# A hybrid decoder step on one core: key chunks, scores and rows in another order

## The reference, cut

```
h = RMSNorm(x);  z = h @ W_in + b_in -> q | k | v | cv_a | cv_g
A = MoBA attention(q, k, v)      8 heads x 64, blocks of 256, own block + the top 3 by q . mean(k)
C = silu(LayerNorm(causal dwconv31(cv_a * sigmoid(cv_g)))) @ W_pw
x = x + RMSNorm(concat[A, C] @ W_out)
u = RMSNorm(x) @ W_up            2 x 2816 wide
x = x + RMSNorm((silu(gate) * val of causal dwconv3(u)) @ W_down)
```

## Time and profile before

| | us |
|---|---|
| median of 3 runs | 1104.83 |
| lowest and highest | 1099.54, 1115.49 |
| the profiled execution's own time | 1101.12 |
| its span | 1099.3 |
| TensorE busy | 972.2 (88%) |
| VectorE busy | 701.6 (64%) |
| ScalarE, GpSimd busy | 444.2, 456.4 |

### The profile page before, as it was taken

How to read it: one execution, slowest core, us unless ns; L and a number is a source line. 1 busy time by engine, 2 the same in 40 slices (tenths; PEclk the granted TensorE clock), 3 DMA queues, 4 the chain that set the end, 5 groups by cost and what they waited for, 6 DMA issues and landing times.

```text
span 1099.3 us, 19605 instructions
## 1 busy us (share of the span) xinstructions
PE 972.2 (88%) x7520; PEld 710.7 (65%) x7520; DVE 701.6 (64%) x920; ACT 444.2 (40%) x892; POOL 456.4 (42%) x408
## 2 busy tenths in 40 slices
PE   3988987889797876977989878999999999999995
PEld 3546663455454444545645558999999999667663
DVE  3689685767665474687432547888888889523115
ACT  3325554656564655444231223333333333234332
POOL 1014445547462848351000335545555545333430
PEclk9998998989897687998999998999999999999998
DMA  9897798997979763787966211232222231222222
GB/s 322 294 320 250 283 332 299 313 358 274 337 260 334 249 216 130 250 283 247 390 181 188 77 39 39 84 103 83 78 78 77 80 113 39 77 77 77 77 73 86
DMA packets 155207, 205.19 MB, mean 187 GB/s; under 512 B 10097, under 2 KB 75634, under 8 KB 155072
## 3 DMA queue, kind: packets, MB, share of 16 engines
q1 hardware_dynamic: 154619, 202.33, 55.1%
q10 hardware_dynamic: 495, 1.62, 0.5%
HBM read 198.59 MB, written 5.68 MB: 186 GB/s over the span
## 4 chain that ended last, share of the span: by engine, by line
PE 63%; SPq 14%; DVE 8%; issue 4%; DMA 4%; ACT 3%; POOL 2%; POOLq 0%; DVEq 0%; ACTq 0%
SPq L326 7%; PE tp L894 7%; PE z L894 6%; PE sc L894 6%; PE z L749 5%; SPq L313 4%; PE ob L894 3%; PE sm L894 3%; PE sc L537 3%; PE tp L925 3%; DMA kN<-in_cache_k 3%; PE ob L925 3%; PE ob L597 2%; PE z L925 2%; PE z L619 2%
## 5 line engine op out<-in xcount | busy, mean ns | idle before, releaser
L1858 POOL TENSOR_TENSOR conv<-conv,prod 128x576 f32<-128x576 f32 x120 | 174.3, 1452 | 143.7 <-ACT prod L1109 130.0
L1453 DVE STREAM_TRANSPOSE kT<-kN 128x2048 f32<-128x2048 f32 x64 | 145.5, 2294 | 52.4 <-DMA kN<-in_cache_k 51.9
L1904 POOL TENSOR_TENSOR wulo<-wu,wuhi 128x2048 fp32r<-128x2048 f32 x22 | 102.3, 4650 | 14.5 <-ACT wuhi L1179 14.5
L1108 ACT ACTIVATE prod<-glu,consts 128x512 f32<-128x512 f32 x124 | 88.9, 717 | 44.8 <-POOL conv L1858 41.8
L1922 POOL TENSOR_TENSOR wdlo<-wd,wdhi 128x1024 fp32r<-128x1024 f32 x22 | 57.4, 2609 | 90.0 <-ACT wdhi L1384 90.0
L537 PE MATMUL sc<-kT,qS 128*32 128x256 f32 x1024 | 70.4, 422 | 26.3 <-DVE kT L1453 23.7
L1763 DVE TENSOR_TENSOR fTlo<-fT,fThi 128x1152 fp32r<-128x1152 f32 x22 | 29.8, 1356 | 91.5 <-ACT fThi L1383 91.5
L632 PE MATMUL z<-hT,wz 128*128 128x512 f32 x192 | 87.1, 607 | 0.0
L597 PE MATMUL ob<-vN,pT 128*32 128x128 f32 x2048 | 75.9, 301 | 0.0
L1043 ACT ACTIVATE S<-sc 128x512 f32<-128x512 f32 x32 | 35.0, 1095 | 98.5 <-PE sc L537 98.4
L597 PEld LDWEIGHTS ob<-vN,pT 128*32 128x32 f32 x2048 | 61.8, 144 | 18.0 <-issue 15.7
(11 more groups left out here) (313 smaller groups left out, 2549.3 us busy)
## 6 DMA issues: line engine op xcount, KB each, us to landing
kN<-in_cache_k SPq DMA_DIRECT2D x256, 256.0 KB, 4.5
vN<-in_cache_v SPq DMA_DIRECT2D x256, 256.0 KB, 4.0
wu<-in_w_up SPq DMA_DIRECT2D x44, 512.0 KB, 4.6
wd<-in_w_down SPq DMA_DIRECT2D x22, 512.0 KB, 3.6
wz<-in_w_in SPq DMA_DIRECT2D x20, 512.0 KB, 6.9
wo<-in_w_out SPq DMA_DIRECT2D x1, 4096.0 KB, 16.4
xA<-in_x_prompt SPq DMA_DIRECT2D x4, 512.0 KB, 11.6
wq<-in_w_in SPq DMA_DIRECT2D x1, 2048.0 KB, 17.6
```

The costliest lines, as they stand in the source:

```text
L1108: act.activation(dst[:, 0:TP_], glu[:, i, j:j + TP_], ACT.Copy, scale=w_cv[:, i, j:j + 1])
L1453: dve.transpose(kT[:, u % 4, :, :].rearrange("p c (i k) -> p i c k", i=4), kN[:, c % 3, :, :].rearrange("p i (c k) -> p i c k", k=32)).the ...
L1858: pool.tensor_tensor(conv[:, i, :], conv[:, i, :], prod[:, n % 2, :], ALU.add).then_inc(s["prod_used"], 1)
L1904: pool.tensor_tensor(wulo[f % 2][:, :, :], wu[f % 2][:, :, :, :].rearrange("p k u n -> p k (u n)"), wuhi[f % 2][:, :, :].bitcast(F32), ALU ...
```

## The change

The order of SyncE's queue: the fourth chunk of keys, 8b+19, is loaded together with 8b+16 to 8b+18, ahead of the values 8b+8 to 8b+11 (at the start 8 to 11 in place of 8 to 10), and keys 8b+13 before values 8b+4. In samples 0 to 3 scores(b+1, 3) follow scores(b+1, 2) directly, at u = 2; ScalarE's copies follow. VectorE turns keys 8(b+2) before the last reduce_scores in place of after penalize; glu_values(2) moves behind that reduction. 106 taps in place of 98 come before sample 4. Of a head's four rows the widest is scaled on VectorE, in p_sums, with a semaphore pnorm_w of its own. Two heads' products with the values run together, alternating between the halves of the partitions (pv_pair), behind the second head's turn. mix_squares(0) stands before exps(7), its root is split off as mix_root, and its sum on VectorE is split off as mix_sum. The order of W_out tiles is 0, 1, 2, 4, 3 (AT); the last turn_out writes bank SC0.

The diff, cut; left out are the same replacement of t by AT[t] in more waits, and mix_sum and mix_root taken out of mix_rows and mix_squares.

```diff
@@ -274,15 +274,17 @@
         wd_full = [s[f"wd_full{i}"] for i in range(4)]
         HEADS_AT = {4: 0, 5: 4}
         XO = (4, 0, 1, 2, 3)
+
+        AT = (0, 1, 2, 4, 3)
         TILES = [(what, i) for i in range(4) for what in "vk"] + [("q", i) for i in range(4)]
         TILES_AT = {1: 0, 2: 4, 3: 8}
-        TAPS_FIRST, TAPS_HEADS = 98, (5, 3, 3)
+        TAPS_FIRST, TAPS_HEADS = 106, (5, 3, 3)
         def scores_at(b):
-            return (0, 2, 2, 3) if b < 4 else (0, 2, 3, 4)
+            return (0, 2, 2, 2) if b < 4 else (0, 2, 3, 4)
...
@@ -357,19 +359,20 @@
             for c in range(4):
                 load_v(c)
             load_wz(2)
-            for c in range(8, 11):
+            for c in range(8, 12):
                 load_k(c)
             rows = lambda n: a[n][0, 0].rearrange("(t p) h d -> p t (h d)", p=P)
             for b in range(NB):
                 if b < NB - 1:
-                    load_k(8 * b + 11)
                     load_k(8 * b + 12)
                 if b < 4:
                     load_wz(2 * b + 3)
+                if b < NB - 1:
+                    load_k(8 * b + 13)
                 load_v(8 * b + 4)
                 if b < NB - 1:
-                    for c in range(8 * b + 13, 8 * b + 16):
-                        load_k(c)
+                    load_k(8 * b + 14)
+                    load_k(8 * b + 15)
                 else:
                     sp.wait_ge(s["kt_ready"], NB * SUPER)
                     sp.dma_start(histF[0:16, :], a["state_ffn"][0].rearrange("b w n -> (b w) n")).then_inc(s["histf_loaded"], 16)
...
@@ -402,7 +405,7 @@
                     sp.wait_ge(s["glun_done"], 2)
                     sp.dma_start(wpw[:, :, :], a["w_cv_pw"][0].rearrange("(k p) n -> p k n", p=P)).then_inc(s["wpw_loaded"], 16)
                 if b < NB - 2:
-                    for c in range(8 * b + 16, 8 * b + 19):
+                    for c in range(8 * b + 16, 8 * b + 20):
                         load_k(c)
                 if b == 6:
...
@@ -600,9 +603,8 @@
             def turn_out(b):
                 pe.wait_ge(s["o_norm"], b + 1)
-                if b == NB - 1:
-                    pe.wait_ge(s["h2_raw"], 3)
-                pe.transpose(TB0[:, 0:P], oN[:, :], ident).then_inc(s["ot_done"], 1)
+                bank = SC0 if b == NB - 1 else TB0
+                pe.transpose(bank[:, 0:P], oN[:, :], ident).then_inc(s["ot_done"], 1)
...
@@ -683,7 +685,8 @@
                     pe.matmul(bank[:, n - P:n], ident16, causal16, start=False, stop=True).then_inc(s["ps_done"], 1)
             def t_head(h):
-                pe.wait_ge(s["pnorm"], 4 * h + 4)
+                pe.wait_ge(s["pnorm"], 3 * h + 3)
+                pe.wait_ge(s["pnorm_w"], h + 1)
                 if h == 0:
                     pe.wait_ge(s["glun_put"], 2)
...
@@ -704,17 +707,20 @@
                 return sum(TP_ - P * i for i in range(kb))
-            def pv_head(h):
-                hp, e = h // 2, h % 2
-                if h == 0:
+            def pv_pair(hp):
+
+                if hp == 0:
                     pe.wait_ge(s["s_put"], 20)
-                if hp and e == 0:
+                else:
                     pe.wait_ge(s["o2_put"], hp)
+                pe.wait_ge(s["ptt_put"], 8 * hp + 8)
                 for kb in range(4):
-                    pe.wait_ge(s["ptt_put"], 4 * h + kb + 1)
-                    ins = pe.matmul(SC1[64 * e:64 * e + 64, kb * P:TP_], vP[:, kb, h * DH:(h + 1) * DH],
-                                    pPT[:, h % 2, turned(kb):turned(kb) + TP_ - kb * P], start=(kb == 0), stop=(kb == 3))
-                ins.then_inc(s["pv2_done"], 1)
+                    for e in range(2):
+                        h = 2 * hp + e
+                        ins = pe.matmul(SC1[64 * e:64 * e + 64, kb * P:TP_], vP[:, kb, h * DH:(h + 1) * DH],
+                                        pPT[:, e, turned(kb):turned(kb) + TP_ - kb * P], start=(kb == 0), stop=(kb == 3))
+                        if kb == 3:
+                            ins.then_inc(s["pv2_done"], 1)
             def statistics(what, done, banks):
...
@@ -734,8 +740,10 @@
             def mix_half(t, nh, part):
                 m = tok(t)
-                if part == 0 and t:
-                    pe.wait_ge(s["t1_put"], 2 * (t - 1) + nh + 1)
+                if part == 0 and t == 3:
+                    pe.wait_ge(s["m4_put"], nh + 1)
+                elif part == 0 and t:
+                    pe.wait_ge(s["t1_put"], 2 * (AT[t] - 1) + nh + 1)
                 if t == 4:
                     for e in range(2):
...
@@ -813,16 +821,14 @@
                     elif u == 2:
                         t_head(h)
                     elif u == 3:
-                        pv_head(h)
                         s_head(h + 2)
                     elif u == 4:
                         t_head(h + 1)
                     elif u == 5:
-                        pv_head(h + 1)
+                        pv_pair(h // 2)
                         s_head(h + 3)
                     elif u == 6:
                         t_head(h + 2)
-                        pv_head(h + 2)
                     elif b == 4:
                         pe.wait_ge(s["pexp"], 16)
                         pe.wait_ge(s["conv_done"], CT)
...
@@ -877,13 +883,14 @@
                             if u == scores_at(b)[j]:
                                 scores(b + 1, j)
                     fill(b, u)
-            mix_half(3, 0, 0)
-            mix_half(3, 0, 1)
             turn_out(NB - 1)
-            mix_half(3, 1, 0)
-            mix_half(3, 1, 1)
-            pe.wait_ge(s["ot_put"], NB)
             h2_tile(2)
+            pe.wait_ge(s["mix_put"], 1)
+            for n in range(4):
+                mix_half(4, n // 2, n % 2)
+            for n in range(4):
+                mix_half(3, n // 2, n % 2)
+            h2_tile(4)
             def up_group(f, n):
                 half, u = n // 2, n % 2
@@ -901,14 +908,10 @@
             pe.wait_ge(s["wu_lo"], 1)
             up_group(0, 0)
             up_group(0, 1)
-            pe.wait_ge(s["mix_put"], 1)
-            for n in range(4):
-                mix_half(4, n // 2, n % 2)
-            h2_tile(3)
             pe.wait_ge(s["wu_lo"], 2)
             up_group(1, 0)
             up_group(1, 1)
-            h2_tile(4)
+            h2_tile(3)
             pe.wait_ge(s["h2_put"], 2 * TT)
             for f in range(2):
                 up_group(f, 2)
...
@@ -1222,9 +1228,9 @@
             put_scores(0, 3)
             spread_q(1)
             gate_exp(1, 0)
-            taps(3)
+            taps(4)
             gate_exp(1, 1)
-            taps(5)
+            taps(6)
             exps(0)
...
@@ -1238,7 +1244,7 @@
                 if b:
                     put_out(b - 1)
                 if b in TILES_AT:
-                    taps(2)
+                    taps(3)
                 put_scores(b + 1, 0)
                 if b == 0:
                     taps(2)
@@ -1248,10 +1254,9 @@
                     taps(1)
                     put_scores(1, 1)
                     put_scores(1, 2)
-                    taps(5)
                     put_scores(1, 3)
                     spread_q(2)
-                    taps(2)
+                    taps(7)
                     gate_exp(3, 0)
                     taps(2)
                     gate_exp(3, 1)
@@ -1264,13 +1269,13 @@
                     taps(2)
                     put_scores(b + 1, 1)
                     put_scores(b + 1, 2)
-                    taps(5)
+                    put_scores(b + 1, 3)
+                    spread_q(b + 2)
+                    taps(4)
                     put_tile(x + 1)
                     if x < 8:
                         put_turned_value(x // 2)
-                    put_scores(b + 1, 3)
-                    spread_q(b + 2)
-                    taps(4)
+                    taps(6)
                     put_tile(x + 2)
                     taps(4)
                     if x < 8:
...
@@ -1328,28 +1333,32 @@
                     for n in range(4, 8):
                         put_pointwise(n)
                     put_scores(7, 3)
+                    mix_squares(0)
                     exps(7)
+            mix_root(0)
             put_turned(7)
             put_out(6)
-            mix_squares(0)
             row_root(0)
             mix_squares(1)
+            mix_root(1)
             row_root(1)
             h2_upper(0)
             mix_squares(2)
+            mix_root(2)
             row_root(2)
             split_up(0)
             h2_upper(1)
             put_out(NB - 1)
             h2_upper(2)
-
-            mix_squares(3)
-            row_root(3)
             split_up(1)
-            h2_upper(3)
             mix_squares(4)
+            mix_root(4)
             row_root(4)
             h2_upper(4)
+            mix_squares(3)
+            mix_root(3)
+            row_root(3)
+            h2_upper(3)
             def put_up(f, half):
...
@@ -1593,8 +1602,11 @@
                 j = 4 * (h % 2)
```

(26 more changed lines are left out.)

58 lines of the change are left out of this document (31 added, 27 removed).

## The result

The kernel after the change took 1137.34 us (median of three, 1129.31 to 1139.34) against 1104.83 us before: a ratio of 1.027 (95% interval 1.021 to 1.033), slower. The forecast was 1109 with a range up to 1133. The profiled execution after took 1137.3 us (span 1135.5), 36.2 more than that of before.

The account below looks back on a forecast made before the run. Bound: a loop through SyncE's one queue in samples 1 to 3, engine waits in samples 4 to 6, TensorE from 660 on. Sum: 1101.1 + 31 - 17 - 4 - 3 + 1 = 1109 us; range 1088 to 1133.

Parts of the forecast that it names:

- the cost of the front: Samples 0 to 3, up to weigh(4,0): longer by 14+6+6+5 = +31 us, ends +12 and +50.
- What bounds the kernel: Samples 1 to 3: a loop through SyncE's one queue, from weigh(b,3) to weigh(b+1,3), closing at 59.4 us in sample 1.
- The loop's length: Samples 1 and 2: from S, the start of scores(b+1,3), to the next, S', 66.2 us against 59.4; +6 each.
- Two edits meet: Samples 0 to 3: scores moved ahead of weigh(b,3) and the early turn make VectorE wait 8 to 15 us, delaying the choice.
- rival B: Front: GpSimd still adds taps, so VectorE's choice stays at 18 us; front about +51, time 1129; chance 0.22.
- Sample 0: glu_values(2) and TensorE's projection group stand behind VectorE's wait for keys 16: values 15 at 207.3, before 193.5; +14 us.
- Eight taps leave sample 4: Sample 4: eight taps of 1.6 us come before it, which removes TensorE's 9.26 us wait for GpSimd.
- Samples 4 to 6: Taps, early keys and pairs of heads shorten them: -17 us in sample 4, -4 in sample 5, -3 in sample 6.
- mix_squares(0): 0: Sample 6: placing mix_squares(0) before exps(7) costs 0, ends -1 and +3 us.
- The end: The way to the up projection: 10 us of TensorE waits go, others replace them; +1 us, ends -2 and +4.
- C: Samples 4 to 6 give little: sample 4 gives -5 in place of -17, 1121 us, or 1128; chance 0.13.
- D: Front: VectorE's wait is covered and the loop runs at 2.9 us a transfer; front +12, 1090 us; chance 0.15.

Follow-up runs that it names:

- weigh_first: The kernel after with scores(b+1,3) behind weigh(b,3) again and ScalarE's order of before: 1090.0 us, ratio 0.983 to before.
- scores_alone: The kernel before with only scores(b+1,3) ahead of weigh(b,3) in samples 0 to 3, and ScalarE's order with them: 1137.72 us, ratio 1.018 to before.
- keys_late: The kernel after with SyncE's key order of before: 1132.36 us, ratio 1.022 to before.
- glu_back: The kernel after with scores(b+1,3) behind weigh(b,3) again and glu_values(2) back before the third reduction: 1078.87 us, ratio 0.971 to before.
- turn_late: The kernel after with VectorE's turn of keys 8(b+2) and glu_values(2) where they were before: 1151.73 us, ratio 1.040 to before.
- taps_alone: The kernel before with only the taps ahead of sample 4 changed, 106 in place of 98: 1098.09 us, ratio 0.989 to before.
- front_of_before: The kernel after with key order, scores in a row, early turn and glu_values(2) all undone: 1090.71 us, ratio 0.985 to before.

## Why the prediction was wrong

The step that failed is the cost of the front, +31 forecast and +55.5 measured. The table counts it at the points of the prediction, the ends of weigh(b,3).

| | before | after | longer | forecast |
|---|---|---|---|---|
| weigh(1,3) ends | 193.5 | 220.6 | +27.1 | +14 |
| from there to weigh(2,3) | 59.4 | 72.2 | +12.8 | +6 |
| from there to weigh(3,3) | 60.6 | 70.9 | +10.3 | +6 |
| from there to weigh(4,0) | 27.9 | 33.2 | +5.3 | +5 |

More than half of what is missing, 13.1 of 24.5 us, is in the chain of sample 0, the rest in the length of the loop.

**What bounds the kernel: right.** The loop that starts at weigh(b,3), goes through the one queue and ends at the scores of the next sample sets the front, before and after. weigh_first and scores_alone show it from both sides.

**The loop's length: right mechanism, mis-sized term.** The step was S' = S + 11.2 + 52.7 + 2.3 = S + 66.2; measured 72.7 and 70.3. In the first of these weigh(1,3) ends at S+12.0 (11.2 taken); from there to keys 31 down are 58.4 us (220.6 to 278.98), where the working had 52.7; the turn is 2.4. The mis-sized term is that of the 16 transfers, 52.7 us: they took 58.4, 3.65 us each and not 3.29. The working's pace (3.35 us) came from a stretch of before that also starts from a pause, as a row of before shows:

```profile
188.00:192.00 4.00, 4.00 (x11) 1.71 (x9) 0.00 (x0) 2.63 (x6) 3.71 (x3) 1.00 0.04 16
```

so the pause alone doesn't explain 3.65; but the two transfers added to it were put at 2.9. Here keys 24 are issued 5.9 us after weigh(1,3) has ended, and their turn begins 8.4 us after that, where 6.4 was taken. The fourth key chunk then waits for that turn; keys_late puts its share at 0.6 to 4.3 us. How the rest divides was not measured. What the working didn't ask is how long the engines stand still in the loop: some 7 us in sample 1 of before (188 to 195), some 10 in after, none in glu_back (a share of 0.85 and more in each 4 us from 186 to 198).

**Two edits meet: half wrong.** The paragraph led with VectorE's wait and with all that stands behind it. The wait came, larger than named (22 to 26 us against "8 to 15"), but has no price of its own: at 11 to 14 us in weigh_first the samples take 60 us, and taking it away (turn_late) makes the kernel slower by 14 us, behind the front. What was wrong in it, and in rival B, is to price a wait by what is queued behind it, without asking whether any of that is what the *bounding* loop waits for. The choice isn't; the slot that weigh(b,3) frees is. The sum itself went by the queue's loop and not by the wait, which is why the front came out longer, as measured. The sign of the whole was right too, but by a net of +8 us on the profiled execution, inside the 22 us that the prediction itself called no change.

**Sample 0: +14 forecast, +27.1 measured at the end of weigh(1,3).** glu_values(2) behind the wait was seen and is a large part: glu_back takes 12.1 us off sample 0 as weigh_first has it. The chain was off from its start. Scores(1,3) ran at 129.0, not 124.9, and this could be read from the trace of before, where keys 14 and 15 are turned by 128.34:

```profile
123.84 4.50 DVE L1453 STREAM_TRANSPOSE kT<-kN 128x2048 f32<-128x2048 f32 x2
```

That is 4.1 us at the start. Keys 16 were issued at 148.4, not 141.7, and their turn began at 156.2, not 148: 8.2 us late. Weigh(1,0) came at 185.3 for 176, S of sample 1 at 208.6 for 196 and the end of weigh(1,3) at 220.6 for 207.3.

**Taps costed at nothing ahead of sample 4: wrong.** "Eight taps leave sample 4" priced only where they leave. taps_alone shows both sides: -14.0 in sample 4 (forecast -9.3) and +8.8 ahead of it (forecast 0; the cover was not named), where the two other runs with that front have +6.5 and +5.3. In sample 0 ScalarE's exponentials stand behind two more taps, and weigh(0,0) behind them: it comes at 100.6 to 103.4 in the twelve kernels with 106 taps, at 99.1 and 99.4 in the two with 98. The net of the taps is not settled (3.4 us by the traces, 12 by the ratio; forecast 9.3).

**Samples 4 to 6.** Sample 4: -17 forecast, -20.7 measured. The taps' part is 14.0 (forecast 9.3). From taps_alone to front_of_before, which has the pairs and the wide row too, are 6.4 us (forecast 6.3), and from there to after and to glu_back, which have keys 43 early, only 0.3 and 1.1 (forecast 2.8). So a term too small and one too large partly made up for each other. The pairs do overlap: one head's 8 matmuls in before and two heads' 16 in after:

```profile
381.94 2.37 PE L715 MATMUL sc<-pPT,vP 128*64 128x512 f32 x8
```

```profile
540.21 2.38 PE L720 MATMUL sc<-pPT,vP 128*64 128x512 f32 x16 [0.47 <-ACT pPT L1155]
```

The wait of 9.26 us is gone. Sample 5: -4, measured -3.9. Sample 6: -3, measured +2.1; what failed is "mix_squares(0): 0": it costs 3.4 us there, though the end gets 2.1 back.

**The end: +1 (ends -2, +4), measured +3.3.** Counted from weigh(7,0), the last up groups of f=0 and 1 start after 99.5 us (696.5 to 597.0), before after 95.5; the step had 95 to 99. In after:

```profile
648.97 6.45 DVE L1770 COPY hT<-oT 64x128 f32<-64x128 f32 x4 [0.86 <-ACT oT L1071]
...
655.47 9.22 PE L751 MATMUL z<-wo,hT 128*64 128x512 f32 x32 [5.87 <-DVE hT L1770]
```

The copies into mixT are done 58.4 us after weigh(7,0), inside the forecast's 56 to 60, though they take 6.45 us and not 5.01. What was too short is a term behind them: the 32 matmuls of tile 4, which come after a wait of 5.87 us, take 9.22 us and not the 7.09 of the earlier trace rows. The granted clock was 0.52 from 655 to 660 in after and 1.00 from 637 to 646, around the same matmuls, in before.

**The rivals.** B named a total (1129; its four terms add up to 52, not 51) near the result for a reason that was not there: the choice took 9.4 us, not 18. Contention is real, though: it was the wait that took the choice out of GpSimd's way. Without the wait (turn_late) the same instructions take 16.1 us. C did not happen: the middle gave 22.5 of the 24 forecast. D was half right: a queue that never runs dry gives samples of 60 us, but the change as made runs it dry. No case had the front at +55: the upper bound of +50 came from the length of the choice, and neither the start of sample 0's chain, nor the pace of the 16 transfers, nor the taps had an upper end.

## What to carry to other kernels

Where one in-order DMA queue is the bound, find the instruction that frees the slot its head waits for, and keep that instruction ahead of everything that the last landed data would also allow; TensorE may be busy all the while and the loss is still whole. A wait costs only what the bounding loop loses by it: ask which of the instructions queued behind it feeds that loop, and move just this one (here glu_values(2), about 11 us) to the other side. A transfer pulled forward in a queue needs the work that frees its buffer pulled forward too (turn_late); the other way round cost nothing here (keys_late).
